# First indices from 64 sums, and two more places for expert rows, in an expert layer fed by gathered rows

## The reference

```python
def peer_ffn(h, w_q, sub_keys, u_tab, v_tab):
    q = (hf @ w_q).reshape(T, PEER_HEADS, 2, PEER_HALF)
    s = jnp.einsum('thpd,hpnd->thpn', q, sub_keys).astype(jnp.float32)
    sv, si = lax.top_k(s, PEER_TOPK)
    cand = sv[:, :, 0, :, None] + sv[:, :, 1, None, :]
    cand_idx = si[:, :, 0, :, None] * PEER_NKEYS + si[:, :, 1, None, :]
    cv, ci = lax.top_k(cand.reshape(T, PEER_HEADS, PEER_TOPK * PEER_TOPK), PEER_TOPK)
    expert = jnp.take_along_axis(cand_idx.reshape(...), ci, axis=-1)
    g = jax.nn.softmax(cv, axis=-1)
    ...
        a = jax.nn.gelu(jnp.einsum('cd,chkd->chk', x_c, u), approximate=False)
        return jnp.einsum('chk,chkd->cd', (g_c * a), vv)
```

## Time and profile before

| | before |
|---|---|
| median of three runs | 1164.13 us |
| the profiled execution | 1164.81 us |
| its span | 1163.0 us |
| row 0 issued | 184.29 us |
| row 1 issued | 191.59 us |
| TensorE's first row matmul | 206.97 us |
| last dot of a row | 840.57 us |
| TensorE busy / VectorE busy | 1033.2 / 814.5 us |

### The profile page before, as it was taken

How to read it: one execution, slowest core, us unless ns; L and a number is a source line. 1 busy time by engine, 2 the same in 40 slices (tenths; PEclk the granted TensorE clock), 3 DMA queues, 4 the chain that set the end, 5 groups by cost and what they waited for, 6 DMA issues and landing times.

```text
span 1163.0 us, 13661 instructions
## 1 busy us (share of the span) xinstructions
PE 1033.2 (89%) x5034; PEld 694.3 (60%) x5034; DVE 814.5 (70%) x1875; ACT 423.1 (36%) x899; POOL 294.1 (25%) x262
## 2 busy tenths in 40 slices
PE   5999999988999886896877778788899999999997
PEld 3798967644555443342333323233389978999986
DVE  6787856777767776888778645545576878888843
ACT  3465713312323222133221211111265666565631
POOL 0000002444454543444544444444000000000000
PEclk9999999999999998998998999999999999999999
DMA  9987694999999999999999999999884344554540
GB/s 377 424 352 312 262 407 180 391 421 421 421 417 422 421 421 422 421 417 421 421 422 421 421 421 421 422 421 422 325 375 181 146 182 150 189 205 176 187 145 36
DMA packets 48343, 390.15 MB, mean 335 GB/s; under 512 B 5515, under 2 KB 6035, under 8 KB 7317
## 3 DMA queue, kind: packets, MB, share of 16 engines
q0 software_dynamic: 37040, 269.51, 56.0%
q1 hardware_dynamic: 11236, 119.77, 26.3%
HBM read 388.20 MB, written 1.06 MB: 335 GB/s over the span
## 4 chain that ended last, share of the span: by engine, by line
PE 53%; DMA 33%; DVE 8%; ACT 3%; issue 2%; POOL 1%; SPq 0%; DVEq 0%; ACTq 0%
DMA ring<-in_uv,idx 30%; PE ps L1510 17%; PE ps L1878 14%; PE ps L2035 5%; PE ps L1535 2%; PE ps L1746 2%; DVE ring L1296 2%; PE ps L1691 2%; PE ps L1963 2%; DMA ring<-in_w_ada 1%; PE ps L1761 1%; DMA ring<-in_w_in 1%; POOL ring L529 1%; DVE ring L928 1%; ACT probT L789 1%
## 5 line engine op out<-in xcount | busy, mean ns | idle before, releaser
L1878 PE MATMUL ps<-ring,probT 128*128 128x512 f32 x1020 | 487.4, 622 | 103.8 <-ACT probT L789 103.7
L1296 DVE CUSTOM_DVE_ANT_0 ring<-h2t,ring 128x1024 f32<-128x1024 f32 x255 | 309.9, 1223 | 184.4 <-DMA ring<-in_uv,idx 182.3
L1878 PEld LDWEIGHTS ps<-ring,probT 128*128 128x128 f32 x1020 | 191.0, 198 | 336.5 <-issue 188.7
L529 POOL DMA_INDIRECT ring<-in_uv,idx x255 | 291.7, 1144 | 339.8 <-PE ps L1878 278.2
L1510 PE MATMUL ps<-util_r,ring_r 128*128 128x256 f32 x1120 | 192.8, 282 | 0.3 <-ACT util L555 0.3
L917 DVE TENSOR_TENSOR ring_r<-ring,ring_r 128x1024 fp32r<-128x1024 f32 (+1 forms) x134 | 155.5, 1204 | 36.0 <-ACT ring_r L551 36.0
L784 ACT ACTIVATE prob<-prob 128x2 f32<-128x2 f32 (+2 forms) x98 | 20.0, 204 | 398.7 <-DVE prob L1296 398.7
L1510 PEld LDWEIGHTS ps<-util_r,ring_r 128*128 128x128 f32 x1120 | 158.1, 188 | 1.3 <-issue 0.7
L551 ACT ACTIVATE ring_r<-ring 128x1024 fp32r<-128x1024 f32 (+1 forms) x134 | 132.0, 1039 | 39.0 <-PE ps L2035 19.1
L1510 PE MATMUL ps<-h_r,ring_r 128*128 128x256 f32 x704 | 125.2, 281 | 0.6 <-DVE util_r L1268 0.6
L789 ACT ACTIVATE probT<-ct,prob 128x128 f32<-128x128 f32 x256 | 85.5, 392 | 86.3 <-DVE prob L1302 83.4
(11 more groups left out here) (225 smaller groups left out, 981.7 us busy)
## 6 DMA issues: line engine op xcount, KB each, us to landing
ring<-in_w_in SPq DMA_DIRECT2D x11, 2048.0 KB, 13.3
ring<-in_w_up SPq DMA_DIRECT2D x11, 2048.0 KB, 8.1
ring<-in_w_ada SPq DMA_DIRECT2D x7, 2048.0 KB, 10.4
ring<-in_w_down SPq DMA_DIRECT2D x6, 2048.0 KB, 8.0
ring<-in_w_ada SPq DMA_DIRECT2D x8, 1024.0 KB, 14.0
ring<-in_w_out SPq DMA_DIRECT2D x4, 2048.0 KB, 8.7
ring<-in_w_q SPq DMA_DIRECT2D x3, 2048.0 KB, 11.6
ring<-in_w_in SPq DMA_DIRECT2D x4, 1024.0 KB, 10.2
```

The lines of the kernel that those rows point to most:

```text
L529: e.indirect_dma_start(out=row_buf[n], out_offset=None, in_=uv, in_offset=bass.IndirectOffsetOnAxis(ap=idx[:, tt, k:k + 1], axis=0)).then_inc(
L1296: e.tensor_tensor_reduce(u, h2t[:, tt, :], u, 1.0, 0.0, ALU.mult, ALU.add, av[:, tt, n % 128:n % 128 + 1]).then_inc(*made.put(("dot", n)))
L1878: ins = e.matmul(acc[half][:, :], diag[:, n % 8, :], row_buf[n][:, D + half * 512:D + (half + 1) * 512], start=(k == 0), stop=(k == 127))
```

## The change

Head 0 of tile 0 gets a search of its own, `first_route`. After the best 8 of both score lists it makes the first index, as before, and then the 64 sums of these 2 x 8 values ("corner"), their best 8, and the indices for rows 1 to 7, with operations of 64 or 128 elements. The rest of the search follows: second best 8 of the lists, all 256 sums with the known 8 taken out, the best 8 of these, indices for rows 8 to 15. The gate weights are split off as `weights`. The scratch of all routes of tile 0 moves from `area` to `h2t[:, 1, :]`, which is filled for tile 1 only once the last route of tile 0 is done.

Two places are added to the rotation: VALUES_BUF (in `area`, behind the queries' place), until row 44, and MERGED_BUF (in `util`), until row 24. For their sake the tile 1 scores of heads 0 and 1 move from row 5 to row 30 on TensorE, and from the batch of row 6 to that of row 32 on ScalarE; the squares of the second norm go to another buffer.

```diff
-FIRST_BUFS = ((0, 1), (2, 0), (2, 1), (1, 0), (1, 1), (3, 0), (3, 1))
-QUERIES_BUF = (NSLOT, 0)
+QUERIES_BUF, VALUES_BUF, MERGED_BUF = (NSLOT, 0), (NSLOT, 1), (NSLOT, 2)
+FIRST_BUFS = ((0, 1), VALUES_BUF, (2, 0), (2, 1), (1, 0), (1, 1), MERGED_BUF, (3, 0), (3, 1))
+LAST_ROW_OF = {VALUES_BUF: 44, MERGED_BUF: 24}
...
         b = LATER_BUFS[n][0] if n in LATER_BUFS else queue.popleft()
+        while n > LAST_ROW_OF.get(b, n):
+            b = queue.popleft()
...
+        bufs[VALUES_BUF] = area[:, 3072:5120]
+        bufs[MERGED_BUF] = util[:, 4096:6144]
...
-                pool.wait_ge(made, ("idx", tt, k // 16) if n else "first idx")
+                pool.wait_ge(made, ("idx", tt, k // 16) if n >= 8 else "first idxs" if n else "first idx")
...
-                elif b == QUERIES_BUF:
+                elif b == MERGED_BUF:
+                    pool.wait_ge(done, ("mix1", 1, 1))
+                elif b in (QUERIES_BUF, VALUES_BUF):
                     pool.wait_ge(done, ("quarter", 39))
...
             def tile_scores(h, tt):
                 act.wait_ge(done, ("scores", h, tt))
+                if tt == 1:
+                    act.wait_ge(done, ("rows", LEFT_AT[MERGED_BUF]))
...
-                    if b0 == 6:
+                    if b0 == 32:
                         tile_scores(h, 1)
...
+            def first_route(mem):
...
+                def picked(name, k0, n):
...
+                    e.tensor_tensor(hot, pos[...], K("iota")[...], ALU.is_equal)
+                    e.tensor_tensor(hot, hot, sif[:, 0:2, 0:n]..., ALU.mult)
+                    e.tensor_reduce(ex[:, 0, k0:k0 + 8], hot..., AX.X, ALU.add)
...
+                steps = top16((*key, "s"), 2, sv, si, s_all[:, 1, 0:2, :], grid...)
+                advance(steps, 2)
...
+                e.tensor_copy(idx[:, 0, 0:1], ex0).then_inc(*made.put("first idx"))
+                e.tensor_tensor(corner..., sv[:, 0, 0:8]..., sv[:, 1, 0:8]..., ALU.add)
+                e.max(cv[:, 0, 0:8], corner)
+                e.max_index(ci[:, 0, 0:8], cv[:, 0, 0:8], corner)
...
+                picked("corner", 0, 8)
+                e.tensor_copy(idx[:, 0, 1:8], ex[:, 0, 1:8]).then_inc(*made.put("first idxs"))
+                advance(steps, 3)
...
+                picked("second", 8, 16)
+                e.tensor_copy(idx[:, 0, 8:16], ex[:, 0, 8:16]).then_inc(*made.put(("idx", 0, 0)))
...
-            routing = (step for group in ROUTES for step in route(*group, area[:, 4096:6144]))
-            advance(routing, 2)
-            first_expert()
-            advance(routing, 12)
+            spare = h2t[:, 1, :]
+            first_route(spare)
+            first_weights = weights(*ROUTES[0])
             rows_added(2, 1)
...
-                if n == 5:
+                if n == 30:
                     for h in range(EARLY_HEADS):
                         tile_scores(h, 1)
```

More of the change, by code:

```diff
@@ L101 @@
 ROW_BUFS = row_buffers()
+LEFT_AT = {b: max(n for n, (c, _) in enumerate(ROW_BUFS) if c == b) for b in LAST_ROW_OF}
 def batch_behind(n):
@@ L713, in tile_queries @@
                 if h >= EARLY_HEADS:
-                    act.wait_ge(done, ("rows", 0))
+                    act.wait_ge(done, ("rows", LEFT_AT[VALUES_BUF] if h >= 6 else 0))
                 e.activation(Q3[:, 2 * h:2 * h + 2, tile[tt]],
@@ L1171, in first_expert @@
                 e.scalar_tensor_tensor(ex0, sif[:, 0, 0:1], 128.0, sif[:, 1, 0:1], ALU.mult, ALU.add).then_inc(
-                    *made.put(("first expert",)))
-                dve.wait_ge(made, ("first expert",))
+                    *made.put("first expert"))
+                dve.wait_ge(made, "first expert")
                 e.tensor_copy(idx[:, 0, 0:1], ex0).then_inc(*made.put("first idx"))
+                e.tensor_tensor(corner.rearrange("p (a c) -> p a c", a=8),
+                                sv[:, 0, 0:8].unsqueeze(2).broadcast_to([P, 8, 8]),
+                                sv[:, 1, 0:8].unsqueeze(1).broadcast_to([P, 8, 8]), ALU.add).then_inc(*made.put("corner"))
@@ new lines, in first_route @@
+                dve.wait_ge(made, "corner")
+                e.max(cv[:, 0, 0:8], corner).then_inc(*made.put("corner max"))
+                dve.wait_ge(made, "corner max")
+                e.max_index(ci[:, 0, 0:8], cv[:, 0, 0:8], corner).then_inc(*made.put("corner at"))
+                dve.wait_ge(made, "corner at")
+                e.tensor_scalar(ch[:, 0, 0:8, 0], ci[:, 0, 0:8], 3, None, ALU.logical_shift_right).then_inc(
+                    *made.put("corner row"))
+                e.tensor_scalar(ch[:, 0, 0:8, 1], ci[:, 0, 0:8], 7, None, ALU.bitwise_and).then_inc(
+                    *made.put("corner col"))
@@ new lines, in first_route @@
+                dve.wait_ge(made, (*key, "cand"))
+                e.match_replace(cand[1], cv[:, 0, 0:8], cand[0], LOWEST).then_inc(*made.put((*key, "rest")))
+                dve.wait_ge(made, (*key, "rest"))
+                e.max(cv[:, 0, 8:16], cand[1]).then_inc(*made.put((*key, "second")))
+                dve.wait_ge(made, (*key, "second"))
+                e.max_index(ci[:, 0, 8:16], cv[:, 0, 8:16], cand[1]).then_inc(*made.put((*key, "at2")))
+                dve.wait_ge(made, (*key, "at2"))
@@ L1220, in route, with weights @@
                 for h in range(h0, h0 + nh):
-                    n0 = 1 if (tt, h) == (0, 0) else 0
-                    e.tensor_copy(idx[:, tt, 16 * h + n0:16 * h + 16], ex[:, h - h0, n0:16]).then_inc(*made.put(("idx", tt, h)))
+                    e.tensor_copy(idx[:, tt, 16 * h:16 * h + 16], ex[:, h - h0, :]).then_inc(*made.put(("idx", tt, h)))
                 yield
+                yield from weights(tt, h0, nh)
+            def weights(tt, h0, nh):
+                key = ("route", tt, h0)
                 g3 = gw[:, tt, 16 * h0:16 * (h0 + nh)].rearrange("p (j n) -> p j n", j=nh)
```

49 lines of the change are left out of this document (41 added, 8 removed).

## The result

| | before | changed |
|---|---|---|
| median of five runs | 1163.85 us (1163.41 to 1164.34) | 1158.68 us (1158.23 to 1159.30) |
| the profiled execution, its span | 1164.81, 1163.0 | 1158.68, 1156.9 |
| last dot of a row | 840.57 us | 834.48 us |
| from the last dot to the end of the span | 322.4 us | 322.4 us |

The ratio is 0.9956, 95% interval 0.9945 to 0.9968: 5.2 us faster by the medians, 3.7 to 6.4 by the interval. A second measurement of the changed kernel, on another chip, gave 0.9949 (0.9936 to 0.9962); one of its six executions took 1296.98 us at a mean granted clock of 0.754, and all comparisons here leave it out. Between the two profiled executions lie 6.1 us, 0.96 more than between the medians; that is the amount by which the profiled execution of before stood above its median.

The account below looks back on a forecast made before the run. The gather was taken as a belt of fixed speed (421 GB/s) bounding the kernel; a lead of 2.1 rows x 2.49 = 5.2 us, other terms costed at nothing, taken from the median 1164.13 gave 1158.9 us, range 1156.8 to 1161.9.

Parts of the forecast that it names:

- The belt: Gather, 234 to 830 us: DMA full at 421 GB/s, 2.49 us a row; the end moves by what is gained before.
- Row 1 earlier: Head 0's search on VectorE: first half takes 2.5 us, so row 1 is issued at 186.8 us, 4.8 earlier.
- The lead of 2.1 rows: Gather's start: the belt gets about 2.1 rows ahead, at 2.49 us each, worth 5.2 us.
- the large case: Lead of 2.4 rows by 212 us; no backlog, so the loss after 212 recurs and the lead falls to two rows.
- VectorE's longer search: Head 0's whole search takes 8.1 us, not 7.3; second tile's additions start 0.8 us later, costed at nothing.
- The cover: ScalarE's table load, 197.65 to 198.93 us, hides VectorE's 0.8 us delay with 0.9 us left; without it, 0.8 cost.
- TensorE's row 0 "still at 207.0": Sign to check: TensorE's first row matmul stays at 207.0 us; if it moves, the prediction is wrong (the cover).
- Issues beside VectorE's dense run: GpSimd issues of rows 1 to 4 beside busy VectorE: at worst 1.99 us each, costing 1.0 us in the lower bound.
- Moved scores: Two score groups (0.89 us) go from TensorE's row 5 to row 30: nothing, at most 0.3 us either way.
- Places given back: Added places end with rows 24 and 44; TensorE has no lag by then, and the state stays 5 us earlier.
- "nothing": Rival: TensorE lags when the two places go, the belt stands 5.0 us and the lead is handed back; 1164, chance 0.06.
- "slower": Rival: scores at row 30 hold up ScalarE's batch of row 32 and all places; 9.8 us lost, 1168.7, chance 0.04.

Follow-up runs that it names:

- first kernel with ten places: Changed kernel with one more 8 KB place in the rotation from row 3 to the end; ratio 0.9960 to the kernel before.
- one index: Changed kernel with rows 1 to 7 fetching the experts of the first index, not waiting for the 64 sums; ratio 0.9962 to the kernel before.
- adds split: Changed kernel with the second tile's row additions halved: behind the first seven indices and inside the rest of the search; ratio 0.9968 to the kernel before.
- two-places kernel: Kernel before with its old search, plus the two added places, moved scratch and moved scores; ratio 0.9985 to the kernel before.
- search alone: Changed kernel with the early search but the old seven places, scores still at row 30; ratio 0.9994 to the kernel before.

## Why the prediction was right

It said 1158.9 us and 5.2 us of gain; measured were 1158.68 and 5.2. Its terms one by one:

- *The belt.* Right, and it is what carries the result: the same 421 GB/s to the end, and the stretch behind the last dot the old 322.4 us. Over thirteen profiles the lead in bytes gives the last dot within 1.2 us.
- *Row 1 earlier.* The search for seven indices was put at 2.5 us and took 186.25 - 183.67 = 2.6, to the operation behind their cast. Issues came at 186.62 (186.8 predicted), 190.38 for row 4 (190.5), 192.71 for row 5 (192.9).
- *The lead of 2.1 rows.* By 212 us 10.4 MB had come in (399 x 26), the large case; then, as the sum said of that case, the weak stretch repeated (370 GB/s) and the lead was (399 x 26 + 370 x 13 - 307 x 26 - 374 x 13) / 1.049 MB = 2.2 rows, 5.6 us. The reason named for it, that row 10 has to wait for row 1's release, is shown by the runs with other numbers of places: no added place 0.7 us, one 3.3, two 5.2 to 5.9, and with three the stretch from 212 to 225 us is full (422 GB/s; 373 in the first kernel with ten places, whose row 0 was late on TensorE).
- *VectorE's longer search.* The additions start 0.9 us later than before, if each is counted from its own row 0 (7.81 and 6.94 us behind it), for 0.8 predicted. That this costs nothing was right in the time and wrong in its reason. The cover was to be ScalarE's table load up to 198.93; in the changed kernel that load ended at 197.72, the chain left it, and VectorE's search and additions are on the chain up to row 0 instead. TensorE waited 0.3 us for them. Row 0 still came earlier than before, since this way is the shorter one.
- *TensorE's row 0 "still at 207.0".* Wrong, by 1.0 us, and the prediction had called itself wrong if that moved. The step that failed takes the table load (197.65 to 198.93) as fixed behind the turned rows' first half. It stands behind ScalarE's copy, which needs only the query matmuls, done by 196.26; in the changed kernel the copy started at 196.04 and the load at 196.44. Why the copy had been a microsecond late is not settled. Rows 8 and 10 came earlier with it (203.15 and 210.11, for 203.7 and 211.1 predicted). The prediction's own row 10, 26.8 us behind row 0, is that of the kernels with one index and with the adds split, which led by 4.5 and 4.9 us; the changed kernel, with 26.1, led by 5.6 and 5.4. So the close agreement of 5.2 us with 5.2 may be in part luck.
- *Issues beside VectorE's dense run.* Rows 1 to 4 took 0.93 to 0.97 us, no more than elsewhere, while VectorE was over nine tenths busy (1.93 of 2 us from 186 to 188). Row 5, beside the additions, took 1.37. The lower bound of 1.0 us for this was not needed.
  The Trainium skill's warning (SBUF — State Buffer, section "SBUF: two separate sides") is for the time in which VectorE holds the shared port pair. Rows 1 to 4 show no such wait, and no row shows whether these operations hold the pair, so the warning is neither borne out nor refuted here.
- *Moved scores.* No run has them alone. They are in the two-places kernel, whose lead of 2.7 us gave 1.7 (0.7 to 2.8), and in the search alone, whose lead of 0.8 gave 0.7 (-0.3 to 1.7). A loss of about 1.1 us or more in them would take the second gain below its interval; a smaller one is not excluded.
- *Places given back.* At rows 24 and 44 nothing is lost (419 to 421 GB/s over the whole stretch); given back at rows 7 and 2 they cost 2.4 to 3.2 us, between the gains of the changed kernel and that run's, measured in other sets. The two rivals that hung on this, "nothing" and "slower", were excluded at these row numbers. The prediction read TensorE's load there from 300 to 400 us, where the kernel before was at about rows 42 to 83 already; from 240 to 300 us TensorE was busy for 53 of 60 us, so the reading holds.
- *Against the profiled execution.* The last dot was to come near 835.4 and came at 834.48. The median of before, not its profiled execution, was the right base for the forecast; the 0.9 us over is the spread of single executions.

## What to carry to other kernels

Where a stream of fixed speed sets the end, count the bytes that it has moved by the time it runs full: that one window says to about a microsecond what a change at its start is worth, before the end is looked at. An earlier start is worth only as much as there are buffers to take what it brings; test start and buffers together, since each alone gave a fraction (0.7 and 1.7 us of more than 5). And a buffer added to a rotation also moves who is last in every slot: look at what loads into those slots next.

## What had not been expected of the hardware

The end of the gather is not that of 16 engines at once. In the ten places kernel, 40 slices from 815 to 840 us (0.625 us each) read

```profile
DMA  9999999999999998553210000000009978999999
GB/s 433 419 419 433 419 419 419 419 419 419 419 419 433 406 393 367 236 210 131 105 79 26 26 26 26 26 26 26 26 0 184 157 275 354 433 406 419 419 433 511
```

For the last 5 us before 833.1 the rate is 26 GB/s, a sixteenth of 421, and then the last dot starts at 833.79. One engine's share of a row is 65,536 bytes, 2.5 us at that rate, and the last five dots follow each other by 2.46 us. (The whole belt's pace, 2.49 us a row, is nearly the same, so the spacing by itself tells little.) This looks like a single DMA engine that is two to three rows behind the rest and on which the last rows' landings wait; the profile doesn't name the engine, and no run tested it. The kernel before has such an end too: from 834 to 839 us its rate is 26 GB/s. So it is not what the change gains or loses.

ScalarE can start about a microsecond after the end of the matmuls that it waits for, as the profile models that end. In three profiles other matmuls followed without a pause and the copy started 0.9 to 1.1 us after the query matmuls' end; in eight TensorE paused, twice because it was made to wait for the copy, and it was 0.03 to 0.05 us. One profile with no pause had it after 0.35 us, and two with a pause after 0.9 and 2.0, so the pause helps and does not decide alone.
